# Low parts of two weight steps by one subtraction on VectorE, in the front of a two-block layer kernel

## What is computed

```python
mod = c_act @ w_ada + b_ada
shift, scale, gate = jnp.split(mod, 3, axis=-1)
h = rms_norm(x, g) * (1.0 + scale[:, None]) + shift[:, None]
proj = jnp.einsum('bsd,df->bsf', h, w_in)
...
y_a = dilated_attention_mixture(q_a, k_a, v_a).reshape(b, s, ATTN_WIDTH)
y_r = bidirectional_retention(q_r, k_r, v_r, dec_f, dec_b).reshape(b, s, RET_WIDTH)
y = jnp.concatenate([y_a * jax.nn.silu(z_a), y_r * jax.nn.silu(z_r)], axis=-1)
out = jnp.einsum('bsf,fd->bsd', y, w_out)
return x + gate[:, None] * out
```

## Time and profile before

| | |
|---|---|
| median of 3 runs | 1481.62 us (1481.25 to 1483.16) |
| span of the profiled execution | 1480.4 us |
| TensorE products busy | 1415.6 us (96%) |
| VectorE busy | 1169.8 us (79%) |
| ScalarE busy | 723.9 us (49%) |
| mean DMA rate | 303 GB/s |

### The profile page before, as it was taken

One profiled execution on the slowest core, in us unless ns is written; L12 is line 12 of the kernel. 1 busy time (PEld: TensorE's weight loads), 2 busy tenths in 40 slices (PEclk: granted clock), 3 DMA queues, 4 the chain that ended last, 5 costly groups with the idle time before them and its releaser, 6 DMA issues.

```text
span 1480.4 us, 19002 instructions
## 1 busy us (share of the span) xinstructions
PE 1415.6 (96%) x6574; PEld 1167.2 (79%) x6574; DVE 1169.8 (79%) x1474; ACT 723.9 (49%) x1039; POOL 116.6 (8%) x217
## 2 busy tenths in 40 slices
PE   4799999999999999999999999999999999999996
PEld 3587777887888778888887888878888888888885
DVE  5999899876999899898767668888788866567566
ACT  4464554554545634444556644464345545565431
POOL 1111011001010011110000100010000000000000
PEclk9999999999999999999999999999999999999998
DMA  9999999877998799999966679669789687555762
GB/s 387 413 414 412 385 362 390 293 258 260 367 416 297 272 405 396 402 376 380 326 233 229 203 251 370 216 238 365 281 339 343 218 296 246 190 189 159 268 198 85
DMA packets 99870, 448.85 MB, mean 303 GB/s; under 512 B 11424, under 2 KB 13776, under 8 KB 76496
## 3 DMA queue, kind: packets, MB, share of 16 engines
q1 hardware_dynamic: 69840, 249.33, 47.2%
q0 software_dynamic: 26352, 185.63, 32.0%
q10 hardware_dynamic: 3600, 12.85, 2.2%
HBM read 445.65 MB, written 2.12 MB: 302 GB/s over the span
## 4 chain that ended last, share of the span: by engine, by line
PE 78%; DVE 12%; DMA 4%; ACT 3%; issue 3%; POOL 0%; SPq 0%; DVEq 0%; ACTq 0%
PE bank L761 22%; PE bank L763 22%; PE bank L762 22%; DVE gw L1466 4%; DVE w_lo L1458 3%; DMA raw<-in_t_steps 2%; PE bank L977 2%; PE bank L927 2%; PE bank L722 1%; PE bank L724 1%; PE bank L723 1%; ACT probs L1122 1%; PE bank L736 1%; DVE area L1466 1%; PE bank L953 1%
## 5 line engine op out<-in xcount | busy, mean ns | idle before, releaser
L1056 ACT CAST w_hi<-raw 128x1024 fp32r<-128x1024 f32 x448 | 469.0, 1050 | 641.5 <-PE bank L763 538.9
L1446 DVE TENSOR_TENSOR w_lo<-raw,w_hi 128x1024 fp32r<-128x1024 f32 x372 | 451.0, 1221 | 249.7 <-ACT w_hi L1056 248.8
L761 PE MATMUL bank<-w_hi,act_hi 128*128 128x512 f32 x1504 | 599.4, 399 | 3.4 <-DVE w_lo L1446 3.4
L762 PE MATMUL bank<-w_lo,act_hi 128*128 128x512 f32 x1536 | 598.2, 389 | 0.0
L763 PE MATMUL bank<-w_hi,act_lo 128*128 128x512 f32 x1504 | 587.1, 390 | 0.0
L1466 DVE CUSTOM_DVE_ANT_0 gw<-gw,c_act 128x2048 f32<-128x2048 f32 x170 | 387.8, 2283 | 3.7 <-DMA gw<-in_t_ada 3.5
L762 PEld LDWEIGHTS bank<-w_lo,act_hi 128*128 128x128 f32 x1536 | 288.8, 188 | 56.9
L761 PEld LDWEIGHTS bank<-w_hi,act_hi 128*128 128x128 f32 x1504 | 282.6, 188 | 61.6 <-issue 3.6
L763 PEld LDWEIGHTS bank<-w_hi,act_lo 128*128 128x128 f32 x1504 | 282.3, 188 | 60.5
L1458 DVE TENSOR_TENSOR w_lo<-raw,w_hi 128x1024 fp32r<-128x1024 f32 x84 | 101.5, 1218 | 16.6 <-ACT w_hi L1056 16.4
L602 POOL DMA_DIRECT2D gw<-in_t_mod x96 | 51.3, 535 | 744.3 <-DVE products L1466 675.5
(11 more groups left out here) (183 smaller groups left out, 987.1 us busy)
## 6 DMA issues: line engine op xcount, KB each, us to landing
raw<-in_t_steps SPq DMA_DIRECT2D x464, 512.0 KB, 5.7
gw<-in_t_mod POOLq DMA_DIRECT2D x96, 1024.0 KB, 7.5
gw<-in_t_ada POOLq DMA_DIRECT2D x42, 1024.0 KB, 8.3
gw<-in_t_kv_mod POOLq DMA_DIRECT2D x32, 1024.0 KB, 8.0
area<-in_t_ada POOLq DMA_DIRECT2D x6, 1024.0 KB, 10.9
area<-gate_rows ACTq DMA_DIRECT2D x3, 1024.0 KB, 12.5
area<-in_ln_g ACTq DMA_DIRECT2D x2, 1024.0 KB, 5.9
area<-in_ln_b ACTq DMA_DIRECT2D x2, 1024.0 KB, 9.0
```

The costliest lines, as they stand in the source:

```text
L761: nc.tensor.matmul(dst, hi, w[:, k], start=(kt == 0), stop=False)
L762: nc.tensor.matmul(dst, hi, w_lo[:, j % SLOTS, k], start=False, stop=False)
L1056: nc.scalar.copy(w_hi[:, b], raw[:, j % SLOTS]).then_inc(hi_ready, 1)
L1446: nc.vector.tensor_tensor(w_lo[:, j % SLOTS], raw[:, j % SLOTS], w_hi[:, j % LEAD].bitcast(F32), ALU.subtract).then_inc(lo_ready, 1)
```

## The change

VectorE's loop in `front` (m = 16 to 83) no longer makes a low part in each half step. In even m it makes none. In odd m one subtraction over two neighbouring slots makes those of steps m - 1 and m, after waiting for the high parts of both, and counts `lo_ready` up by 2 when it is done. The rest of each half step keeps its order. Head, later stages and all other engines are untouched.

```diff
+            def split_two_lows(n):
+
+                j, b = n % SLOTS, n % LEAD
+                dve.wait_ge(hi_ready, n + 2)
+                nc.vector.tensor_tensor(w_lo[:, j:j + 2], raw[:, j:j + 2], w_hi[:, b:b + 2].bitcast(F32),
+                                        ALU.subtract).then_inc(lo_ready, 2)
+
...
                     if step:
                         scores_step(*step)
-                    split_low(m)
+                    if m % 2:
+                        split_two_lows(m - 1)
                     kt, late = divmod(m - HEAD_STEPS, 3)
```

## The result

The changed kernel takes 1490.24 us, median of 4 runs (1488.66 to 1491.0), against 1482.39 for the kernel before on the same chip (4 runs). The ratio is 1.0050, 95% interval 1.0037 to 1.0062: 7.4 us slower, 5.5 to 9.2.

The account below looks back on a forecast made before the run. TensorE bounds the whole kernel, with VectorE's order counting where TensorE waits. Step 42's 2.2 us lateness grows through buffers to 5.8 at step 65, less 0.62 hidden: 5.2 on 1481.6 gives 1486.8 us, range 1482.0 to 1490.5.

Parts of the forecast that it names:

- The saving: VectorE, steps 16 to 83: 34 double subtractions replace 68, saving 0.07 us each, 2.4 us in all.
- An even step loses one step of its lead: Steps 16 to 83: from high-part release to low-part need, an even step has two steps (5.4 us), not three (8.2).
- The start of the sum at step 42: Step 42 waits for the high part of 43, set by an unmoved arrival at 160.20: TensorE 2.2 us late.
- the prediction's own signs: Wrong if step 42 is not late, arrivals before 166 us move over 1 us, or TensorE waits behind 290 us shrink.
- slower still: Rival, 10%: earlier row-product loads displace a weight step, 2.5 us more, 1489.3 us.
- The way back through the buffers: Late releases delay high parts of 47 and 51; VectorE is 2.6 us late at 183.5, step 61 5.9 late.
- The first rival: Rival, 22%: VectorE's entry to 180.93 is not late, so lateness does not come back through the buffers; 1484.1 us.
- Behind step 65: After step 65 VectorE has slack; TensorE's 0.62 us wait at 252.93 is hidden, and 5.2 us lateness stays to the end.
- The faster rival: Rival, 8%: VectorE's chain shortens from 166 to 250 us and TensorE stalls before 166 shrink; 4.4 us faster, 1477.2 us.

Follow-up runs that it names:

- two singles with the same joint wait: Changed kernel with both low parts made in the odd half step by two subtractions, both starting only when both high parts are there; ratio 1.0037 against the kernel before.
- two singles and own waits: Changed kernel with both low parts made in the odd half step by two subtractions, each waiting for its own high part; ratio 1.0020 against the kernel before.
- the second execution: The changed kernel run once more with nothing altered, against the kernel before; 1489.53 us, ratio 1.0045.
- the kernel with early pairs: Changed kernel with pairs only for steps 16 to 39, and steps 40 to 83 by one subtraction each; ratio 1.0021 against the kernel before.
- pairs only in the full stretch: Changed kernel with pairs only for steps 52 to 65, all other steps by one subtraction each; ratio 1.0018 against the kernel before.

## Why the prediction was right, and where its size was off

**The saving.** 0.07 us a pair was forecast. The double subtraction takes 2.29 us with the next start 2.21 behind it (144.77 to 146.98), and VectorE's busy time fell by 1.8 us in all. Right, and it bought nothing: two singles with the same joint wait lost less, 1.0 us less by step 20 alone.

**An even step loses one step of its lead.** Right. The kernel with two singles and own waits shows the place alone (3.8 late at 79), the joint wait adds 2.0 to 2.5.

**The start of the sum at step 42.** This term was mis-sized: 2.2 forecast, 5.0 and 3.4 measured. I wrote that losses before 136 us are taken up in the waits behind it, that the last step set by an arrival is 43, and that its arrival is unmoved. In the changed kernel the arrival of 43 sets nothing: its weights were there at 158.5 us, 1.7 before the 160.18 of the kernel before, and ScalarE waits for TensorE:

```profile
161.22 1.05 ACT L1056 CAST w_hi<-raw 128x1024 fp32r<-128x1024 f32 x1 [1.66 <-PE bank L724]
```

What sets it is the lateness that comes in: 2.5 us by step 34, and the wait at step 36, which is itself an arrival met by a pair. The weights of 37 came at 143.6, 2.3 us later than before, and the old kernel's waits at 38 and 39 took up only part of it. With steps 36 to 39 made singly, or all steps before 40, the term was 3.2 and 2.9. By the prediction's own signs, an arrival before 166 us that moves by more than 1 us stood against it, and these two did.

Part of the later arrival of 37 may be the change's. SyncE issued its load at 126.70 where it was 124.78, because TensorE finished step 29 1.9 us later:

```profile
126.70 0.33 SPq L558 DMA_DIRECT2D raw<-in_t_steps  x1
```

But the load of 36 was issued as much later and landed only 0.1 later, and in the six kernels with nothing changed before step 40 the weights of 37 landed anywhere from 140.6 to 144.5 us. So the cause of the 2.3 us stays open, and with it the rival "slower still", whose 1489.3 lies nearest to the measured time: no run separates earlier row-product loads from the rest.

**The way back through the buffers.** Right in mechanism, the size following the first term. VectorE's double subtraction of 50 and 51 left it free at 186.3 (forecast 183.5, 2.8 early, as step 43 was). From there to the share of 60 and 61 it took 35.4 us (221.7), forecast 35.3. Step 61 follows 60 by one step of TensorE, 2.80 us, as forecast. So the stretch adds 4.0 to what comes in (forecast 3.7): 9.0 from 5.0 here, 6.9 from 2.9 and 7.2 from 3.2 in two others (8.9 from 3.4 in the second execution, with the half clock inside it). The first rival, lateness without the way back, needed VectorE back at 180.93 and is out by the 186.3. One row was misread: the high part of 47 at 167.2 in the kernel before waited for its weights, which landed at 167.19, and not for TensorE, which was done with step 43 at 167.0. The two lie so close that the sum does not change.

**Behind step 65.** 0.6 was to be hidden; 1.0 was (8.9 to 7.9 at step 79, 1.0 to 1.1 in the others that have the change in steps 52 to 65). The rest stayed to the end, as said.

**The sum.** The forecast's 2.2 + 3.7 - 0.1 - 0.6 = 5.2 became 5.0 + 4.0 - 0.1 - 1.0 = 7.9 in the profiled execution, and 7.4 by the ratio. The mechanism of the long stretch held; the time stayed inside the range by only 0.3 us, and that is luck, since the first term alone was 2.8 off.

**What was not in the forecast.** The 2.5 us lost before step 34, which were to be taken up later; TensorE's waits before steps 54 and 56; the fall of the clock, about 1.5 us where it fell; and that softmax operations queued behind the joint wait cost time where TensorE itself has lead. I named them as queued, and priced them at nothing.

The faster rival, and with it the first half of the rule of the Trainium skill ("Perfetto Trace Analysis", section "Optimizing Scalar/DVE Operations", group where VectorE is saturated), did not hold here: in the one stretch where VectorE was 98% busy, pairs alone cost 2.7 us. The rule's second half, to break up what holds others up, agrees with the trace: two singles with their own waits cost less than pairs (3.0 against 7.4 us). Of "VectorE: DVE Perf Modes", section "The TRN2 errata", the length of the double subtraction agrees (2291 ns by its formula, 2289 measured), the estimate of 157 ns saved for each merging, which I worked out from it, does not.

## What to carry to other kernels

Merging two instructions of a producer moves the first result to the time of the second, and makes it wait for the second's inputs. Before merging, compare for each even item when the odd one was ready and when the consumer took the even one: in the kernel before, the low part of step 39 was ready at 153.05 us and step 38 had begun at 149.37, and that difference of 3.7 us was the warning. It does not rank the losses: for 36 and 37 it was only 1.8 us (143.64 and 141.87), and the largest single wait came there, because in the changed kernel the second input arrived 2.3 us later. Where producer and consumer share few buffers, count what the lateness does to the next release. And look at what is queued behind the new wait, even where the consumer has lead.

## What the runs showed of the hardware

TensorE's granted clock fell to 1.2 GHz for some 6 us at the end of a wait of 3.53 us (products 0.43 us apart from 147 to 153 us), and again with waits of 3.40 us in the kernel with early pairs and of 3.37 in the one with the joint wait. It did not do so each time: after a like wait of 3.46 us in the second execution of the changed kernel it stayed at 2.4 GHz. Shorter waits were sometimes followed by some 3.4 us at half clock: 2.12 us before step 56 with pairs only in the full stretch, and 2.28 us before step 60 in the second execution of the changed kernel, while in its first execution the same wait of 2.28 us was not. So the length of the wait alone does not say whether the clock falls.

Two subtractions of 1024 columns back to back take 2.27 us of VectorE and one of 2048 takes 2.21. So merging saved 0.06 us a pair.
